# RWKV-7 chunk inverses of a six-layer model: T negated and updated in place by masked copies, transposed on TensorE, and the end of the layer done by halves of the tokens

## The reference, cut to what matters

```python
    def step(state, inp):
        r_t, w_t, k_t, v_t, kk_t, a_t = inp
        sa = jnp.einsum('bhvk,bhk->bhv', state, kk_t)
        state = (state * w_t[:, :, None, :]
                 - sa[..., None] * (kk_t * a_t)[:, :, None, :]
                 + v_t[..., None] * k_t[:, :, None, :])
        return state, jnp.einsum('bhvk,bhk->bhv', state, r_t)
    ...
    y = jnp.moveaxis(y, 0, 1)
    mu = jnp.mean(y, axis=-1, keepdims=True)
    var = jnp.mean(jnp.square(y - mu), axis=-1, keepdims=True)
    y = ((y - mu) * lax.rsqrt(var + RW_GN_EPS)).reshape(B, S, D) * ln_w + ln_b
    y = y + (jnp.sum(rh * kh * r_k, axis=-1, keepdims=True) * vh).reshape(B, S, D)
    out = (y * g).astype(h.dtype) @ w_out
```

## Time and profile before

| | us |
|---|---|
| median of 3 runs | 1935.93 |
| lowest and highest | 1933.72, 1939.68 |
| the profiled execution's own time | 1935.0 |
| its span from first to last instruction | 1932.9 |
| PE busy | 1817.4 (94% of the span) |
| DVE busy | 1263.3 (65%) |
| ACT busy | 1029.7 (53%) |
| POOL busy | 146.0 (8%) |
| matmul instructions on PE | 18871 |

### The profile page before, as it was taken

How to read it: one execution, slowest core, us unless ns; L and a number is a source line. 1 busy time by engine, 2 the same in 40 slices (tenths; PEclk the granted TensorE clock), 3 DMA queues, 4 the chain that set the end, 5 groups by cost and what they waited for, 6 DMA issues and landing times.

```text
span 1932.9 us, 43768 instructions
## 1 busy us (share of the span) xinstructions
PE 1817.4 (94%) x18871; PEld 1631.5 (84%) x18871; DVE 1263.3 (65%) x1783; ACT 1029.7 (53%) x1585; POOL 146.0 (8%) x106
## 2 busy tenths in 40 slices
PE   6987999999989999898999999998899999998998
PEld 5887788889979888887698888887798888887887
DVE  6875367865436675486668856876467755775764
ACT  5834455554535554354655545744465554564455
POOL 0051100000000000014000000151100000000000
PEclk9999999999989999899899999999999999998999
DMA  6420145557576655355465562320245555443441
GB/s 190 132 86 4 53 146 184 190 182 244 174 233 217 197 191 180 110 174 178 150 198 184 186 204 93 120 76 4 68 153 191 178 188 169 134 146 104 152 132 66
DMA packets 288535, 287.92 MB, mean 149 GB/s; under 512 B 15240, under 2 KB 286456, under 8 KB 288344
## 3 DMA queue, kind: packets, MB, share of 16 engines
q1 hardware_dynamic: 285048, 284.02, 45.8%
q10 hardware_dynamic: 3296, 1.11, 0.3%
HBM read 284.06 MB, written 1.05 MB: 148 GB/s over the span
## 4 chain that ended last, share of the span: by engine, by line
PE 90%; DVE 4%; issue 3%; ACT 2%; DMA 0%; POOL 0%; SPq 0%; DVEq 0%; ACTq 0%; POOLq 0%
PE ps L419 23%; PE ps L420 12%; PE ps L401 10%; PE ps L403 9%; PE ps L402 9%; PE ps L814 3%; PE ps L436 2%; PE ps L437 2%; PE ps L438 2%; PE ps L713 1%; PE ps L784 1%; PE ps L798 1%; PE ps L675 1%; PE ps L641 1%; PE ps L727 1%
## 5 line engine op out<-in xcount | busy, mean ns | idle before, releaser
L463 DVE TENSOR_TENSOR wl<-raw,wh 128x1024 fp32r<-128x1024 f32 x484 | 596.5, 1251 | 345.4 <-ACT wh L453 340.9
L453 ACT ACTIVATE wh<-raw 128x1024 fp32r<-128x1024 f32 x484 | 499.4, 1041 | 432.0 <-PE ps L420 191.2
L419 PE MATMUL ps<-HH,wh 128*128 128x512 f32 x1408 | 489.7, 391 | 0.0
L420 PE MATMUL ps<-HH,wl 128*128 128x256 f32 x1408 | 397.0, 282 | 0.0
L419 PEld LDWEIGHTS ps<-HH,wh 128*128 128x128 f32 x1408 | 264.3, 188 | 55.6 <-issue 0.4
L401 PE MATMUL ps<-HH,wh 128*128 128x256 f32 x928 | 271.4, 292 | 10.2 <-DVE HH L2498 5.5
L420 PEld LDWEIGHTS ps<-HH,wl 128*128 128x128 f32 x1408 | 266.1, 189 | 0.1
L402 PE MATMUL ps<-HH,wh 128*128 128x256 f32 x928 | 263.6, 284 | 0.0
L403 PE MATMUL ps<-HH,wl 128*128 128x256 f32 x928 | 263.3, 284 | 0.0
L401 PEld LDWEIGHTS ps<-HH,wh 128*128 128x128 f32 x928 | 179.3, 193 | 20.8 <-issue 6.6
L402 PEld LDWEIGHTS ps<-HH,wh 128*128 128x128 f32 x928 | 179.6, 193 | 1.2 <-issue 1.2
(11 more groups left out here) (323 smaller groups left out, 3119.6 us busy)
## 6 DMA issues: line engine op xcount, KB each, us to landing
raw<-in_ffn_w_gu_dram SPq DMA_DIRECT2D x88, 1024.0 KB, 5.1
raw<-in_ffn_w_down_dram SPq DMA_DIRECT2D x32, 1024.0 KB, 5.1
raw<-in_w_in_dram SPq DMA_DIRECT2D x32, 1024.0 KB, 5.4
raw<-in_rw_w_rkv_dram SPq DMA_DIRECT2D x24, 1024.0 KB, 5.3
B<-in_w_ada_dram SPq DMA_DIRECT2D x24, 1024.0 KB, 7.7
raw<-in_ds_w_in_dram SPq DMA_DIRECT2D x14, 1024.0 KB, 5.3
raw<-in_ffn_w_down_dram SPq DMA_DIRECT2D x16, 768.0 KB, 4.4
raw<-in_sb_w_qkv_dram SPq DMA_DIRECT2D x12, 1024.0 KB, 5.5
```

The source lines that it names most:

```text
L419: e.matmul(o[:, m, :], h_[:, k, c], x_, start=k0 + k == 0, stop=False, skip_group_check=True)
L420: i = e.matmul(o[:, m, 0:S], l_[:, k, c], x_[:, 0, :], start=False, stop=k0 + k == kt - 1, skip_group_check=True)
L453: e.activation(wh[:, u % UNITS, 0:kn * 256], raw[:, j % RAW, k0 * 256:(k0 + kn) * 256], ACT.Copy).then_inc(*up("hi"))
L463: e.tensor_tensor(wl[:, u % UNITS, 0:kn * 256], raw[:, j % RAW, k0 * 256:(k0 + kn) * 256], wh[:, u % UNITS, 0:kn * 256].bitcast(F32), ALU. ...
```

## The change

The inverse is now written with the signs turned: what is kept is -T, whose lower blocks are filled in place. `At` (buffer 1) is an unmasked copy of the gram matrix `bp` on ACT. Buffer 6 starts as minus the identity (ACT, `clear`), and DVE's `copy_predicated` puts the elements of a product into T only where the mask `low{m}` of the level is not zero. The layout of T is `(j q h t)`, so that a 128 x 128 tile holds two heads of two chunks. A level is now: the product `xs` = At with T (64 matmuls), copied by ACT without a mask; 16 transposes of T itself (`turned`) into `Tw`, copied by ACT; and one product `low` = Tw with X1 (64 matmuls), copied by DVE under the mask. The third product of each level is gone. The last level (m = 32) has `xs` copied under its mask into a buffer of identities (`Xw`) and the product `tt` that gives the transposed inverse. GpSimd has no part in the inverses any more, and the gram `bq` (32 matmuls) is gone.

TensorE's order around it: each projection of values is cut in its two units, one ahead of `second_products` and one behind; so is `full(0, 1, 3)`. Its result stays in bank 0 (`kept_bank`), and the rest of this stretch takes turns over seven banks (`cur["first"] = 1`). The grams and transposes after the levels are in another order.

At the end, centring, squares, averages, Ln, Exp, the multiplications, rounding and the low parts are done for 128 tokens at a time: the first half's `cen` and `var` stand ahead of and behind `from_state(3)`, and `gate(0)`, `gate(1)` stand one chunk earlier.

```diff
@@ constants
-    add("nm1", ...)
-    add("nm1T", ...)
-    for m in LEVELS:
-        add(f"lv{m}", ... & (sc % (2 * m) < m) & (tc % (2 * m) >= m))
+    for m in (1, *LEVELS):
+        add(f"low{m}", ... & (sc % (2 * m) >= m) & (tc % (2 * m) < m))
@@ pe_rwkv
+            def turned(m, j):
+                for r in range(2):
+                    o = bank(e, ("turn", n, m, j, r), ("act", ("turn", n, m, j, r)))
+                    for q in range(4):
+                        i = e.transpose(o[:, q * P:q * P + P], BUF[6][:, (8 * j + 4 * r + q) * P:...], ident)
+                    i.then_inc(*up("mm", ("turn", n, m, j, r)))
             def first_products(m):
...
+                for j in range(2):
+                    for a in range(2):
+                        e.wait_ge(*at("act", ("bp", n, j, a)))
+                        e.wait_ge(*at("dve", ("low", n, m // 2, j, a)))
+                    quarters("xs", m, j, At, T, "dve" if m == 32 else "act")
+                for j in range(2):
+                    turned(m // 2, j)
             def second_products(m):
...
-                    if m != LEVELS[-1]:
-                        quarters("t", m, pair, s_in, straight, Tt, X1, now_by)
-                    quarters("tt", m, pair, s_in, s_out, X1, Tt, now_by)
+                        e.wait_ge(*at("dve" if m == 32 else "act", ("xs", n, m, j, a)))
+                        e.wait_ge(*at("act", ("turn", n, m // 2, j, a)))
+                    if m == 32:
+                        quarters("tt", m, j, Xw, Tw, "act")
+                    else:
+                        quarters("low", m, j, Tw, X1, "dve")
...
-            gram("bq", 1, Bt_, Pm, 1)
-            full(0, 1, 3)
-            first_products(2)
+            last_read = block_halves(0, 1, 3)
+            next(last_read)
             if n:
...
+            next(last_read)
             for g in range(4):
-                full(2, 0, g)
+                first_products(LEVELS[g])
+                values = block_halves(2, 0, g)
+                next(values)
                 second_products(LEVELS[g])
-                if g < 3:
-                    first_products(LEVELS[g + 1])
+                next(values)
@@ act_rwkv
-                e.wait_ge(*at("dve", ("bp read", n, j, par)))
-                e.activation(Bt[:, j, par, :], PS("bp", n, j, par)[:, :], ACT.Copy)...
+                copy_out(("bp", n, j, par), At[:, j, par, :])
             hi(e)
...
+            e.activation(BUF[0][:, :]..., C("eye")..., ACT.Copy).then_inc(*up("act", ("eye", n)))
+            evac(0, 3, R_)
             for g in range(4):
+                for j in range(2):
+                    quarters_out("xs", LEVELS[g], j, X1)
+                hi(e, 1)
+                turned(LEVELS[g] // 2)
                 hi(e, 1)
                 if n == 0:
                     evac(2, g, v_)
@@ dve_rwkv
+            def level(key, m, dst):
+                for j in range(2):
+                    for a in range(2):
+                        e.wait_ge(*at("mm", (key, n, m, j, 1)))
+                        e.copy_predicated(dst[:, j, :, a, :], low8(m), q8(PS(key, n, m, j, a)[:, :])).then_inc(...)
...
             for g in range(4):
+                if n and g:
+                    value_mix(g - 1)
                 lo(e, 1)
                 if g == 0:
-                    read_decay(0)
-                    read_decay(1)
+                    key_decay(0)
+                    key_decay(1)
...
+                level("low", LEVELS[g], T)
+                lo(e, 1)
@@ pe_rwkv, the end (ACT and DVE likewise by halves t of the tokens)
             new_y(1)
+            gate(0)
+            gate(1)
             keys_values(1, 1)
             y_values(1)
             from_state(2)
             new_state(2)
             new_y(2)
-            gate(0)
-            gate(1)
+            centred(0)
             from_state(3)
+            spread(0, 0)
+            spread(0, 1)
+            new_y(3)
             gate(2)
-            new_y(3)
+            centred(1)
+            spread(1, 0)
+            spread(1, 1)
             gate(3)
@@ pool_rwkv: the loops of lines 2759 to 2770 are gone
```

More of the change, by code:

```diff
@@ L386, in halves, with fm_unit @@
             return (w_[:, u % UNITS, 0:kn * 256].rearrange("p (k n) -> p k n", k=kn) for w_ in (wh, wl))
+        def fm_unit(e, key, o, kt, k0, kn, u, src, ready):
+            e.wait_ge(book.sems["lo"], u + 1)
+            h_, l_ = halves(u)
+            for m in range(2):
+                c = slice(m * P, m * P + P)
+                om = o[:, m * S:(m + 1) * S]
+                for k in range(kn):
+                    if ready is not None and m == 0:
+                        for ev in ready[k0 + k]:
+                            e.wait_ge(*at(*ev))
+                    xh_, xl_ = src(k0 + k)
+                    e.matmul(om, h_[:, k, c], xh_, start=m == 0 and k0 + k == 0, stop=False, skip_group_check=True)
+                    e.matmul(om, h_[:, k, c], xl_, start=False, stop=False, skip_group_check=True)
+                    i = e.matmul(om, l_[:, k, c], xh_, start=False, stop=k0 + k == kt - 1, skip_group_check=True)
+            i.then_inc(*up("unit", *([key] if k0 + kn == kt else [])))
         def fm_block(e, key, kt, src, ready, *free):
@@ L872, in pe_rwkv @@
                 pe_to_tm(e, ("V", n, j), v_, j)
-            first_products(32)
             for j in range(2):
-                gram("br", j, Bt_, R_)
-            second_products(32)
+                gram("kr", j, Kp, R_)
+            for j in range(2):
+                pe_to_tm(e, ("bTM", n, j), Bt_, j)
             for j, par in groups:
@@ L883, in pe_rwkv @@
             for j in range(2):
-                pe_to_tm(e, ("bTM", n, j), Bt_, j)
-            for j in range(2):
-                gram("kr", j, Kp, R_)
-            for j in range(2):
                 pe_to_tm(e, ("kTM", n, j), Kp, j)
@@ L996, in new_y, with centred, spread @@
                 from_u(c, "y", ("y", n, c), u_tile, br_tile)
+            Y = FM(6)
+            def centred(t):
+                for m in range(2):
+                    if t == 0 and m == 1:
+                        cur["bank"] += 2
+                    o = bank(e, ("cen", n, t, m), ("dve", ("cen", n, t, 2 * m + 1)))
+                    e.wait_ge(*at("act", ("y", n, 2 * t + 1)))
+                    e.matmul(o[:, :], C("cent"), Y[:, 4 * m:4 * m + 4, t * P:t * P + P], start=True, stop=True,
+                             skip_group_check=True).then_inc(*up("mm", ("cen", n, t, m)))
+            def spread(t, m):
+                o = bank(e, ("var", n, t, m), ("act", ("var", n, t, m)))
+                e.wait_ge(*at("act", ("ysq", n, t, m)))
+                e.matmul(o[:, :], C("bavg"), ysq[:, 4 * m:4 * m + 4, :], start=True, stop=True,
+                         skip_group_check=True).then_inc(*up("mm", ("var", n, t, m)))
             own_values(0)
@@ L2346, in dve_rwkv, with weighted, gated, rest_y @@
             e.wait_ge(*at("mm", ("tt", n, 32, 1, 1)))
+            gw = FM(7)
+            def weighted(t, g):
+                c = slice(2 * g, 2 * g + 2)
+                o = PS("cen", n, t, g // 2)[:, g % 2 * S:g % 2 * S + S]
+                e.wait_ge(*at("mm", ("cen", n, t, g // 2)))
+                e.wait_ge(*at("act", ("gate", n, g)))
+                if g % 2 == 0:
+                    e.wait_ge(*at("act", ("ysq", n, t, g // 2)))
+                e.tensor_tensor(Y[:, c, t * P:t * P + P], two(o), gw[:, c, t * P:t * P + P], ALU.mult).then_inc(*up("dve", ("cen", n, t, g)))
+            def gated(t, g):
+                tk, c = slice(t * P, t * P + P), slice(2 * g, 2 * g + 2)
+                yg = Y[:, c, tk]
+                e.wait_ge(*at("act", ("yrn", n, t, g // 2)))
+                e.wait_ge(*at("dve", ("cen", n, t, g)))
+                e.tensor_tensor(yg, yg, yrn[t][:, c, :], ALU.mult).then_inc(*up("dve"))
+                e.wait_ge(*now("dve"))
+                e.tensor_tensor(yg, yg, term[:, c, tk], ALU.add).then_inc(*up("dve", ("gated", n, t, g)))
+            def rest_y(t, g):
+                tk = slice(t * P, t * P + P)
+                dve_lo_part(e, Y[:, 2 * g:2 * g + 2, tk], tuple(pair(x, g)[:, :, tk] for x in (XH, XL)), ("act", ("yh", n, t, g)),
+                            ("yl", n, g) if t else ("yl first", n, g))
             negate_u(0)
@@ L2351, in dve_rwkv @@
             next_state(1)
+            gate_term(0)
             negate_u(2)
```

327 lines of the change are left out of this document (138 added, 189 removed).

## The result

The changed kernel takes 1942.91 us (median of 20 runs, 1935.96 to 1950.23) against 1934.17 us (20 runs, 1930.53 to 1941.22) for the one before. The ratio is 1.0042 with a 95% interval of 1.0032 to 1.0053: 0.4% slower, about 8 us, where 1922 us and faster was forecast. The profiled execution took 1942.9 us with a span of 1940.8.

What follows compares the result with a forecast made beforehand. TensorE, busy 1817 of 1933 us, was taken as the bound, with open time mostly in "issue" gaps. Layer n = 0 gave -8.3, n = 1 0, the end -8.4, clock falls +2.6: -14.1, so 1922 us, whole range 1905 to 1935.

Steps and rivals of the forecast that it cites:

- The stall: In each level TensorE waits 2.15 us before `low`, for ACT's turned copies queued behind `hi`.
- The end: From y to the output projection: centring and gating by token halves saves 4.2 us a layer, 8.4 in all.
- The gaps and the work: TensorE's work stays equal (9.7 us dropped, 9.6 added), 12.05 a level; "issue" gaps shrink to 5 us or so.
- Rival 4: Gaps come with each run of small matmuls, whatever lies between: time 1945 us; chance 0.05.
- The masked copies: DVE's copies into T under the mask take 0.6 us each, so TensorE does not wait for them.
- rival 3: DVE's masked copies set the level; at 1.5 us each the time is 1943 us; chance 0.08.
- the levels: Inverse steps in both layers: 14.2 us each with TensorE's wait, but 18.1 for the first of n = 1.
- two falls in eight levels: TensorE's clock falls behind the levels' waits only twice, at 1.3 us each: +2.6 us.
- rival 1: The clock falls in every level, price 8 x 1.3 = 10.4 us: time 1930 us; chance 0.12.
- The tail: Behind the levels up to `tp`: six small runs and five of transposes, 22.4 us, plus about 3 of gaps.
- The start of the layers: From the grams to the first level: -1.0 us in n = 0; 17.2 us long in n = 1.

Runs made afterwards that it cites:

- e2: The changed kernel with the end of the layer as before, over all 256 tokens, so that the inverses alone are changed: 1947.6 us.
- e11: e8 with the end of the layer as before: 1908.3 us.
- e3: The kernel before with the new end by token halves and nothing else: 1930.2 us, ratio 0.9972.
- e8: e7 with the first half of projection `full(0, 3)` between the Gram products `pb` and `bp`: 1899.7 us.
- e1: The changed kernel with ACT's four copies of the turned T ahead of the `hi` that waits for the half projection, in each level: 1924.6 us.
- e5: e1 with DVE's decay and own-term work ahead of the waiting `lo` in every level: 1914.9 us.
- e4: The changed kernel with each of ACT's four copies of the turned T made twice: 1964.4 us.
- e6: e1 with ACT's work ahead of the first level reordered, and v2 products and sigmoids behind the first level's first products: 1916.7 us.
- e10: e8 with ACT's `hi` again ahead of the turned copies in seven of the eight levels: 1924.0 us.
- e7: e1 with the edits of e5 and e6, and `value_mix(3)` behind the last level's masked copies: 1905.3 us.

## Why the prediction was wrong

The stall, the vanishing gaps and the shorter end that it saw were there. Three terms of the sum were too small, above all the falls of the clock, and they outweighed the gain. Measured from the profiled executions (1935.0 and 1942.9 us), the difference is +7.9 us against a forecast of -14.1: 22 us to explain.

**The end: right in the traces.** -8.4 forecast; by the traces of the two kernels about 4 us in each layer, by those of e2 and e11 6.4 and 7.0 in both together. The medians say 3.9 (e3), 4.7 (e2) and 8.6 (e11) and can't decide between half and all of it.

**The gaps and the work: right.** A level's 12.05 us is exact (e8, and the second level above). The "issue" gaps fell to 8 us in n = 0. Rival 4 (gaps with each run) did not come: of the eight runs of 128 in the levels of n = 0 one has a gap, of 0.88 us. e8 shows that the same reading, used on the grams, is worth 10.6 us in the stretches and 5.6 in the median.

**The masked copies: right.** 0.72 us is the median of 40, 0.64 from one to the next in a queue, against 0.6. No wait for them shows in the levels of the changed kernel, and 2.5 us in all in the steps behind them; rival 3 did not come.

```profile
L2305 DVE COPY_PREDICATED B<-CT,ps x40: 707/724/746, 120.2 to 1342.3; 128x512 f32<-128x512 int32 x40
```

**The step that failed: the levels.** They took 134.8 us together where the sum had 122.3 (56.8, 0.2, 18.1, 42.6, 2 of gaps, 2.6 of clock). The prediction said "I count two falls in eight levels, +2.6". There were seven, and they cost 10.5 us (e1), +7.9 over the forecast. That is rival 1, with its price of 8 x 1.3 = 10.4 nearly exact, at a chance of 0.12. What went wrong was the weighing: two gaps of before were at hand, one of 1.86 us after which the clock held and one of 2.45 after which it fell, and a forecast wait of 2.15 was put on the side of the first. The wait was 2.49. ACT starts `hi` 0.09 us behind the end of the half projection (115.62), and TensorE goes on some 0.3 us behind the second copy: hand-overs of 0.4 us where the sum had 0.1. With the one of 2.58 the difference is 2.8 us over eight levels. The other waits in the levels (0.3 to 0.9 us in some, and those of the first level of n = 1) come to 5.6 us, half a microsecond under the 6.1 that the sum had for them. Another 2.2 us are busy time of TensorE: e1's eight levels, at full clock, have 98.6 us of it where the sum had 96.4.

The length of a wait alone does not say whether the clock falls. Before the grams of n = 1 TensorE waits 1.83 us in five kernels; behind it the clock stays at 1.00 in the changed kernel, e2 and e5, and is at 0.54 and 0.55 in e1 and e4. Waits of 2.12 us (changed kernel) and 2.11 us (e1) in the first level of n = 1 kept it, and so did one of the eight of 2.49. So no run shows that 2.15 us would have spared the levels; what the runs show is that these waits, as they were, brought seven falls and not two.

The rule of the Trainium skill named in the prediction ("TensorE: Matmul & The Clock Gate", "Part 4: PE-mode transpose": transposes don't count as busy) would have led to these falls. e1 and e8 have the same transposes and a clock of 1.00 over all the levels, so the transposes alone do not bring them. Whether they help a wait to do it was not tried.

**The tail, +6.1 us.** 28.9 and 28.0 us from the last `xs` to `tp`, 25.4 forecast for each (22.4 and 3 of gaps). 3.7 of it is `G`, in two layers: "six small runs (6 x 2.12)" counted it among the products that take 2.15 us for 128 records, and it takes 3.95 (30.9 ns a record against 16.8). It is the same product as before, and the trace of before has it with 3.24 us for 104 records (at 187.28).

**The start of the layers, +5.5 us.** In n = 0 the gap in the grams stayed and grew from 2.45 to 3.27, with a wait for a bank of 0.60 and a longer stretch at half clock behind it, where -1.0 was forecast. In n = 1 (its first level took 19.4 us, 18.1 forecast, which counts among the levels) the grams wait 1.83 us for the bank that `evac(0, 2)` frees. Ahead of it stand ACT's two new copies `clear` (2.1 us, the second after a wait of 1.6 for DVE) and two `hi`, the second of which waits for TensorE itself; with `evac(0, 2)` ahead of that one the wait is 0.69 us (e6). What the copies cost by themselves was not tried. The forecast placed them in ACT's idle time and didn't follow who stood behind them.

12.5 in the levels (7.9, 2.8 and 2.2, less 0.5, with rounding), 6.1 and 5.5 are 24.1 us; the end is 0.2 worse in the traces, and outside the two layers the profiled execution was 2.3 us shorter: 22.0.

**The chances.** The terms failed all in one direction, and the range (to 1935) allowed for each alone. Rival 1 was priced at 1930 since everything else was kept; with the tail and the start it would have been 1942. (Rival 3's time is 1944 by its own terms, 1922 + 22, and the 0.3% of its condition are reached at c = 1.43; nothing hangs on either.) The second stall, of DVE's decay work behind a waiting `lo`, was hidden by the first and came to light in e1 alone (7.1 us).

## What to carry to other kernels

In a queue written by hand, an instruction that waits for the engine it feeds (here `hi`, for a free weight slot) goes behind everything that this engine waits for next, and fill-in work goes ahead of it: two exchanges of order were worth 18 and 6 to 13 us, and made a change that was 0.4% slower 1.1% faster. Where the trace shows the clock falling after waits like the new one, price each occurrence with the fall (here 2.5 + 1.0 to 1.5 us), not without it. In this kernel short matmuls ran with few gaps where some 3 us of projection stood between runs of 128; and the row of every product is read by itself, since two of the same count can differ by a factor of 1.8.

## What the runs showed of the hardware

- Behind a wait of TensorE of 2.49 us (2.58 twice) its clock went from 1.00 to one half (1.2 of 2.4 GHz) for a while in 7 of 8 levels of the changed kernel, and in e10 behind 6 of 7 such waits; in the same levels without the wait (e1, e8) it stayed at 1.00. It is not certain each time: the level from 124.64 to 139.19 us had the wait and the full clock.
- The same wait of 1.83 us before the grams of n = 1 was followed by a clock of 1.00 in the changed kernel, e2 and e5 and of 0.54 and 0.55 in e1 and e4: the length of one wait does not settle it.
- 128 small matmuls with all four combinations of input and output halves take 2.15 us; `G`, whose output half is always its input half, takes 3.95. No run changes this order alone.
- 256 small matmuls in a row had a gap of 1.0 to 3.3 us in them (changed kernel, e1, e6, e7); in two runs of 128 with 24 matmuls of 128 x 256 between, none in n = 0 and 0.9 us in n = 1 (e8), where the next run of 128 had one of 1.0 us.
- A masked copy (COPY_PREDICATED) of 128 x 512 out of PSUM takes 0.72 us, of which 0.64 count in a queue.
